# HGRN score products regrouped: the diagonal product ahead of the retention updates, levels 0 to 3 in one run, levels 4 to 6 in another

## The reference, cut to what matters

```python
b = jnp.cumsum(lfc, axis=-2)
diff = b[:, :, :, None, :] - b[:, :, None, :, :]
decay = jnp.exp(jnp.where(causal, diff, -jnp.inf))
scores = jnp.einsum('bhid,bhjd,bhijd->bhij', qc, kc, decay)
```

## Time and profile before

| | |
|---|---|
| median of 3 runs | 1402.32 us (1402.03 to 1403.26) |
| the profiled execution | 1402.38 us |
| its span | 1400.6 us |
| PE busy | 1383.8 us (99%) |
| DVE, ACT, POOL busy | 999.3, 483.7, 368.1 us |
| mean granted TensorE clock | 0.998 |

### The profile page before, as it was taken

The page is one execution under the profiler, slowest core; times in us unless marked ns, Lnnn a source line. Parts: engine busy times, 40 slices in busy tenths (PEclk is TensorE's granted clock), DMA queues, the critical chain, the costliest instruction groups (busy, mean ns, idle before and its releaser), DMA issues.

```text
span 1400.6 us, 24702 instructions
## 1 busy us (share of the span) xinstructions
PE 1383.8 (99%) x10042; PEld 1165.8 (83%) x10042; DVE 999.3 (71%) x1330; ACT 483.7 (35%) x842; POOL 368.1 (26%) x292
## 2 busy tenths in 40 slices
PE   7999999999999999999999999999999999999997
PEld 5788898889888988898889888988898888888886
DVE  5555676667689889988898889877676768532345
ACT  4323243234333333342334333333333344221234
POOL 0000114311532153215321532153206225201220
PEclk9999999999999999999999999999999999999999
DMA  9994442435343535454444454433443357182235
GB/s 387 418 418 161 117 126 69 120 72 139 95 161 108 172 94 178 111 153 119 161 116 140 128 166 114 130 97 106 106 106 86 103 151 278 53 305 93 90 106 210
DMA packets 207735, 212.40 MB, mean 152 GB/s; under 512 B 144256, under 2 KB 156816, under 8 KB 202768
## 3 DMA queue, kind: packets, MB, share of 16 engines
q1 hardware_dynamic: 207600, 210.89, 47.9%
q10 hardware_dynamic: 32, 0.02, 0.0%
HBM read 182.27 MB, written 24.40 MB: 148 GB/s over the span
## 4 chain that ended last, share of the span: by engine, by line
PE 95%; DMA 3%; DVE 1%; SPq 0%; issue 0%; ACT 0%; DVEq 0%; ACTq 0%
PE ps L2122 10%; PE ps L2124 10%; PE ps L2123 10%; PE ps L1957 9%; PE ps L1958 8%; PE ps L1959 8%; PE ps L1933 8%; PE ps L2299 5%; PE ps L2301 5%; PE ps L2300 5%; DMA area<-in_w_mod 2%; PE ps L2139 2%; PE ps L1964 2%; PE ps L1965 2%; PE ps L1966 2%; PE ps L1923 2%
## 5 line engine op out<-in xcount | busy, mean ns | idle before, releaser
L1201 DVE TENSOR_TENSOR w_lo<-area,w_hi 128x1024 fp32r<-128x1024 f32 x143 | 190.3, 1331 | 206.7 <-ACT w_hi L729 206.7
L729 ACT ACTIVATE w_hi<-area 128x1024 fp32r<-128x1024 f32 x143 | 151.5, 1059 | 495.5 <-PE ps L2124 266.1
L2122 PE MATMUL ps<-w_hi,hT_hi 128*128 128x512 f32 x640 | 251.1, 392 | 0.0
L2124 PE MATMUL ps<-w_hi,hT_lo 128*128 128x512 f32 x640 | 249.1, 389 | 0.0
L2123 PE MATMUL ps<-w_lo,hT_hi 128*128 128x512 f32 x640 | 249.0, 389 | 0.0
L1957 PE MATMUL ps<-hT_hi,w_hi 128*128 128x512 f32 x512 | 204.8, 400 | 0.0
L1958 PE MATMUL ps<-hT_lo,w_hi 128*128 128x512 f32 x512 | 199.7, 390 | 0.0
L1959 PE MATMUL ps<-hT_hi,w_lo 128*128 128x512 f32 x512 | 199.6, 390 | 0.0
L2124 PEld LDWEIGHTS ps<-w_hi,hT_lo 128*128 128x128 f32 x640 | 120.1, 188 | 25.2
L2122 PEld LDWEIGHTS ps<-w_hi,hT_hi 128*128 128x128 f32 x640 | 120.2, 188 | 24.3
L2123 PEld LDWEIGHTS ps<-w_lo,hT_hi 128*128 128x128 f32 x640 | 120.2, 188 | 24.1
(11 more groups left out here) (282 smaller groups left out, 2427.7 us busy)
## 6 DMA issues: line engine op xcount, KB each, us to landing
area<-in_w_in SPq DMA_DIRECT2D x144, 512.0 KB, 4.2
area<-in_w_mod SPq DMA_DIRECT2D x26, 1024.0 KB, 12.3
area<-in_w_out SPq DMA_DIRECT2D x38, 512.0 KB, 3.9
gate_raw<-in_w_gate SPq DMA_DIRECT2D x32, 512.0 KB, 4.0
gate_raw<-in_w_mod SPq DMA_DIRECT2D x6, 1024.0 KB, 12.1
o_hi_scratch<-area SPq DMA_DIRECT2D x56, 80.0 KB, 2.4
o_lo_scratch<-area SPq DMA_DIRECT2D x56, 80.0 KB, 2.4
hT_hi<-o_hi_scratch SPq DMA_DIRECT2D x14, 320.0 KB, 7.0
```

The lines of the kernel that those rows point to most:

```text
L729: act.activation(split_weights(h, n)[0], raw[:, n % 3, :], ACT.Copy).then_inc(wt_hi.sem, 1)
L1201: v.tensor_tensor(lo, raw[:, n % 3, :], hi.bitcast(F32), ALU.subtract).then_inc(wt_lo.sem, 1)
L2122: mm(out, hT_hi[:, k, tile_cols(t)], w_hi[:, n % 2, w], start=k == 0, stop=False)
L2124: i = mm(out, hT_lo[:, k, tile_cols(t)], w_hi[:, n % 2, w], start=False, stop=k == KT - 1)
```

## The change

- Product 0 goes behind chunk 0, ahead of the retention updates (`own_scores`), and is placed at DVE's item 0 (`place_own`) instead of item 4. PE waits for that placing ahead of the retention outputs.
- Levels 0 to 3 are one run behind chunk 5 (`early_scores`), levels 4 to 6 one behind chunk 8 (`late_scores`). The gate's four matmuls go ahead of the first run.
- Level 0 uses two matmuls of 64 x 64 a tile in place of four of 32 x 64.
- Levels 2 to 6 and the diagonal are written packed to PSUM (32 columns a tile), and placed by one instruction that repeats them over a tile.
- Each level has a buffer of its own (`decayed`), in areas that belong to retention and key buffers: level 1 in `KL`, 3 in `rqd` and `kts`, 4 and 5 in `ktl`, `rS` and `rope`. So the writers of those wait for the last product (`pe_level`) of the head before, and SP loads the retention states at 14 instead of 6.
- The differences of levels 1 / 2, 3 / 4, 5 / 6 are made at items 3 / 4 / 6 / 7, where they were at items 4 (1, 2), 6 (3, 4) and 8 (5, 6). ACT's exponentials are at 4 (1, 2), 5 (3), 6 (4, 5), 7 (6), the query decays at 4 (1), 5 (2, 3), 7 (4, 5), 8 (6). Placings are at items 6 and 9.
- The last head keeps its single products, with level 0 in the new form.

```diff
+DIFFERENCES = {3: (1,), 4: (2, 3), 6: (4, 5), 7: (6,)}
+OWN_DECAYS = {4: (1,), 5: (2, 3), 7: (4, 5), 8: (6,)}
+DECAYS = {4: (1, 2), 5: (3,), 6: (4, 5), 7: (6,)}
+SCORED, EARLY_PRODUCTS = (5, 8), 5
+PACKED, PACK = 2, TILES * QUAD
...
+        decayed = {0: XE[:, 0], 1: KL, 2: halves(area[:, XE0 - T:XE0 + 5 * T])[:, :, 0:T], 3: halves(area[:, RET1:RET1 + 2 * T]),
+                   4: halves(area[:, KTL0:KTL0 + 2 * T]), 5: halves(area[:, KTL0 + 2 * T:KTL0 + 4 * T]), 6: XE[:, 0]}
...
-                if n == 6 and h is not None:
+                if n == 14 and h is not None:
...
-                    if due(pe_ro, h - 1):
-                        sp.wait_ge(pe_ro.sem, pe_ro.at(h - 1))
+                    if due(pe_level, h - 1):
+                        sp.wait_ge(pe_level.sem, pe_level.at(h - 1))
...
-                        sp.wait_ge(roped.sem, roped.at(h - 1))
+                        sp.wait_ge(pe_level.sem, pe_level.at(h - 1))
...
-                if due(pe_level, h, level):
+                if following is not None and level:
+                    dve.wait_ge(pe_hu.sem, pe_hu.at(h))
+                    if level == LEVELS - 1:
+                        dve.wait_ge(pe_level.sem, pe_level.at(h, EARLY_PRODUCTS))
+                elif due(pe_level, h, level):
...
+            def place_own(h):
+
+                dve.wait_ge(pe_level.sem, pe_level.at(h, 1))
+                scores = ps[:, A, 0:PACK].rearrange("p (t n) -> p t n", n=QUAD).unsqueeze(2).broadcast_to([P, TILES, P // QUAD, QUAD])
+                v.tensor_copy(hsT.rearrange("p (t b n) -> p t b n", t=TILES, n=QUAD), scores).then_inc(h_sT.sem, 1)
...
             def gate_reduced(h):
 
                 b = gate_block(h)
+                pe.wait_ge(h_S.sem, h_S.at(h))
+                pe.wait_ge(h_state.sem, h_state.at(h))
...
-                for c_ in range(4):
-                    if level == 0:
-                        partners = slice(P // 2, P) if c_ < 2 else slice(0, P // 2)
-                    else:
-                        partner = c_ ^ 1 if level == 1 else c_
-                        partners = slice(partner * QUAD, (partner + 1) * QUAD)
-                    rows = slice(c_ * QUAD, (c_ + 1) * QUAD)
+                size = P // 2 if level == 0 else QUAD
+                for c_ in range(P // size):
+                    partner = c_ ^ 1 if level <= 1 else c_
+                    partners = slice(partner * size, (partner + 1) * size)
+                    rows = slice(c_ * size, (c_ + 1) * size)
...
+            def run_scores(h, following, levels):
+
+                for level in levels:
+                    pe.wait_ge(la.sem, la.at(h, level + 2))
+                    pe.wait_ge(lq.sem, lq.at(h, level + 1))
+                    q, keys = level_queries(following, level), level_keys(following, level)
+                    for t in range(TILES):
+                        if level < PACKED:
+                            i = tile_scores(level, ps[:, A, tile_cols(t - 1)] if t else ps[:, DD, 0:P], keys[:, tile_cols(t)], q[:, tile_cols(t)])
+                        else:
+                            i = packed_tile_scores(packed_scores(level)[:, t * QUAD:(t + 1) * QUAD], keys[:, tile_cols(t)], q[:, tile_cols(t)])
+                    i.then_inc(pe_level.sem, 1)
...
                     if n == 0:
+                        own_scores(prev)
                         retention_updates(prev)
                     if n == 1:
+                        pe.wait_ge(h_sT.sem, h_sT.at(prev, 1))
                         retention_outputs(prev, A, BB)
                         chunk_updates(prev)
-                    if n == 3:
-                        level_scores(prev, h, 0)
-                        level_scores(prev, h, 1)
-                    if n in (5, 7, 9):
-                        level_scores(prev, h, n - 3)
-                        if n == 5 and 0 <= gate_block(prev) < GATE_BLOCKS:
+                    if n == SCORED[0]:
+                        if 0 <= gate_block(prev) < GATE_BLOCKS:
                             gate_reduced(prev)
-                        level_scores(prev, h, n - 2)
+                        early_scores(prev, h)
+                    if n == SCORED[1]:
+                        late_scores(prev, h)
```

More of the change, by code:

```diff
@@ L959, in items @@
                     context_columns(h)
-                if prev is not None and n in (4, 6, 8):
-                    decays(prev, n - 3)
-                    decays(prev, n - 2)
+                if prev is not None:
+                    for level in DECAYS.get(n, ()):
+                        decays(prev, h, level)
                 if n == 11:
@@ L1032, in _ @@
             items(CHUNKS - 1, last, None)
-            decays(last, 0)
+            decays(last, None, 0)
             tokens_context(last)
@@ L1475, in chunk_states, with place_packed @@
                     dve.wait_ge(h_S.sem, h_S.at(h, i + 1))
-            def place(h, following, product):
-                scored, placed = pe_level.at(h, (product if following is None else product | 1) + 1), h_sT.at(h, product)
+            def place_packed(h, levels):
+                quads = hsT.rearrange("p (t b n) -> p t b n", t=TILES, n=QUAD)
+                for level in levels:
+                    placed = h_sT.at(h, level)
+                    if not isinstance(h, int):
+                        placed = dve.to_reg(placed)
+                    dve.wait_ge(masks_in.sem, masks_in.at(0))
+                    dve.wait_ge(h_sT.sem, placed)
+                    where = mask(level).rearrange("p (b n) -> p b n", n=QUAD).unsqueeze(1).broadcast_to([P, TILES, P // QUAD, QUAD])
+                    scores = packed_scores(level).rearrange("p (t n) -> p t n", n=QUAD).unsqueeze(2).broadcast_to([P, TILES, P // QUAD, QUAD])
+                    v.copy_predicated(quads, where, scores).then_inc(h_sT.sem, 1)
@@ L1482, in place, with place_late @@
+            def place_late(h):
+                scored = pe_level.at(h)
+                if not isinstance(h, int):
+                    scored = dve.to_reg(scored)
+                dve.wait_ge(masks_in.sem, masks_in.at(0))
+                dve.wait_ge(pe_level.sem, scored)
+                place_packed(h, range(EARLY_PRODUCTS - 1, LEVELS))
+            def place(h, product):
                 if product:
                     dve.wait_ge(masks_in.sem, masks_in.at(0))
-                dve.wait_ge(pe_level.sem, scored)
@@ L1524, in items @@
                         retention_turn(prev)
[L1525 to L1536, removed]
+                    for level in DIFFERENCES.get(n, ()):
+                        differences(prev, h, level)
+                    for level in OWN_DECAYS.get(n, ()):
+                        own_decay(prev, h, level)
+                    if n == 0:
+                        place_own(prev)
+                    if n == SCORED[0] + 1:
+                        place_early(prev)
+                    if n == SCORED[1] + 1:
+                        place_late(prev)
                     if n == 4:
@@ L1673, in _ @@
             hgrn_silu(last, 0)
-            place(last, None, 3)
-            differences(last, 4)
+            place(last, 3)
+            differences(last, None, 4)
             hgrn_silu(last, 1)
@@ L1691, in _ @@
             hgrn_silu(last, 3)
-            place(last, None, 7)
+            place(last, 7)
             hgrn_silu(last, 4)
@@ L1885, in _ @@
             last = HEADS - 1
-            key_decay(last, 0)
+            key_decay(last, None, 0)
             key_factors(last)
             for level in range(1, LEVELS):
-                differences(last, level)
-                key_decay(last, level)
+                differences(last, None, level)
+                key_decay(last, None, level)
             pool.wait_ge(fnw_in.sem, fnw_in.at(0))
```

235 lines of the change are left out of this document (134 added, 101 removed).

## The result

The changed kernel takes 1409.86 us (median of 5 runs, 1409.2 to 1411.51) against 1402.32 before: a ratio of 1.0056, 95% interval 1.0044 to 1.0067. It is slower by 7.5 us, more than twice what can be told from no change, and 3.9 us above the upper end of my range. The profiled execution took 1411.51 us with a span of 1409.7, so its span is 9.1 us longer than before.

What follows compares the result with a forecast made beforehand. PE's own instruction stream was taken as the bound. Its -0.45 us plus 0.4 of stall came to about 0 against the median of 1402.32, so the forecast was 1402.2 us, range 1398.5 to 1406.0.

Steps and rivals of the forecast that it cites:

- the new waits: Whether operands reach PE late at the new places, followed in head 4: 0.4 us of stall in all.
- a key decay: POOL's key decay per level, taken as 2.5 us, so POOL is done at 650.6, 0.9 ahead of level 3.
- the diagonal run: Product 0 on PE ahead of the retention updates, priced at 0.69 us per head with a predecessor.
- The stall: PE waiting for late operands in heads 3 to 6: 0.1 us each, bounds 0 and 2.0 each.
- Rival 3: DVE's query decays of levels 2 and 3 late in heads 3 to 6, 2.0 us each: 1410; chance 0.15.
- PE's price list: PE's score costs: 0.40 us a product, 0.29 a run beside its products, level 0 0.61.
- The early run: Levels 0 to 3 on PE: 2.25 us, seen as about 2.4 from weight matmul to weight matmul.
- the late one: Run of levels 4 to 6 on PE: 1.49 us, seen as 1.6 from weight matmul to weight matmul.
- rivals 1 and 4: Level 0 at 0.31 and inner changes free, 1397.9, chance 0.18; wide strips not overlapping, 1406.6, chance 0.05.
- The inner change of width: Switch between 64-wide and 32-wide strips inside a run on PE: 0.15 us, bounds 0 and 0.29.
- Rival 2: Changes of width drain in full, 0.29 us for each of eleven inner changes: 1403.7; chance 0.12.
- PE's stream: PE's own instruction cost: 0.15 us saved per head, 1.05 in seven, 0.6 back for the gate, -0.45 in all.

Runs made afterwards that it cites:

- x1: Changed kernel with POOL making the key differences of levels 2 and 3 ahead of level 1's key decay: 1401.91 us against 1402.77, ratio 0.9994.
- x3: Changed kernel with DVE's gate step behind item 3 on 8 columns in place of 512, leaving out part of the gate's sum: 1401.48 us, ratio 0.999.
- x9: Changed kernel with DVE's gate step of item 3 ahead of level 1's differences instead of behind them: 1409.86 us, ratio 1.0055.
- x4: Changed kernel with the run of levels 0 to 3 behind chunk 6 in place of chunk 5, its placing one item later: 1408.38 us, ratio 1.004.
- x6: Kernel before the change with only level 0 altered, to two matmuls of 64 stationary columns a tile: 1403.41 us, ratio 1.0007.
- x2: Changed kernel with ACT's exponential of level 2 moved from item 4 to item 5, behind the rounding of chunk 6: 1420.29 us, ratio 1.0124.
- x8: Changed kernel with POOL's differences ahead of its key decay, narrow level 0, and the diagonal product in the early run: 1407.66 us, ratio 1.0039.
- x10: Changed kernel with POOL's differences ahead of its key decay, narrow level 0, and level 3 in the late run: 1404.01 us against 1402.73, ratio 1.0005.

## Why the prediction was wrong

**The step that failed** is in the new waits: "a key decay is 1.20+1.33 = 2.5", with POOL done by 650.6, and from it that ACT's split of chunk 6 waits "to about 645.4, still ahead of DVE". The key decay of level 1 took 5.20 + 0.87 = 6.1 us, as it started beside DVE's unbroken series; ACT's rounding came at 649.9, DVE's split at 650.9, the query decays of levels 2 and 3 from 652.8 to 655.6. In the prediction's own time (1.57 us less) the rounding is at 648.3, 2.9 later than said, and the key decay ends at 645.7 where I had 641.4. Of these 4.3 us, 3.6 are its duration. The other 0.7 is a slip of mine: I took the clocks of head 4 from the before trace and left out the 0.69 of the diagonal run that the change puts ahead of them. The stall I took as 0.1 per gate head, with bounds 0 and 2.0. It measured 1.9, so the upper bound held and the middle did not. I had put a mean duration on an instruction whose neighbour I had just placed beside it: the means of the earlier trace rows come from a schedule in which POOL's key decays met DVE at other moments. x1 takes the wait away by order alone, x3 by taking the gate step away, which moves DVE's series against POOL's start; x9 shows that DVE's end and not POOL's start sets the end, and x4 that ACT's queue carries the loss.

**Rival 3** named the right wait (query decays of levels 2 and 3, heads 3 to 6, 2.0 each, 1410) by the wrong mechanism. It had POOL slow down every DVE step, and I held against it that POOL waits in part of the stretch. DVE was not slowed in the series, where its differences took 0.48; it then stood idle for 5.28 us behind an engine that it had kept out itself. Only from 650.94 on did it run slow beside POOL: 1.90 us for the split in place of 1.22, and 1.44 for each query decay in place of 0.81, 1.9 us in all. That alone makes no wait, as in x1 and x3 the two decays are as slow (2.90 us together) and PE never waits; but with the idle time before it, it adds to how late levels 2 and 3 are. With a chance of 0.15 on the right number, the range should have reached it.

**PE's price list was right.** The diagonal run, said 0.69, is seen in head 2, laid beside the earlier trace rows. From the last query matmul (331.68, the second record of the first line) to the first scan matmul it takes 0.76; less that chunk's step of 0.15, with the 0.07 behind it, that is 0.68:

```profile
331.53 0.46 PE L1996 MATMUL ps<-hT_hi,w_lo 128*128 128x320 f32 x2
331.92 0.56 PE L2267 MATMUL ps<-area 128*32 128x32 f32 x40
332.44 0.91 PE L2213 MATMUL ps<-area 128*128 128x128 f32 x6
333.18 0.39 PE L2214 MATMUL ps<-area 128*128 128x128 f32 x2
```

The six records behind it take 0.74, as in the tail. The early run, said 2.37, took 2.35, the late one, said 1.61, took 1.62; a wide pair of level 0 in the tail comes every 0.058 us, so time goes by the rate of a strip (rivals 1 and 4 fall, the tail's run went from 1.02 to 1.05). The inner change of width, said 0.15, is at most 0.11 (x6). Rival 2, and with it the reading of the Trainium skill's rule on changing the tiling mode (TensorEngine Tiling (Array Packing), Key Properties) that charged a whole 0.29, falls too: an inner change costs under half of that. PE's stream saved 0.24 to 0.28 per plain head where I had 0.15; 0.04 of that is the inner change, the rest, under 0.1, I can't name. In x1, without the waits, it is 0.17 to 0.19, and the gate heads (138.57 to 138.73 us) save nothing, as the sum had it.

**Without the wait the forecast holds.** x1 is the change with POOL's list put in another order: its ratio of 0.9994 makes 1401.5 us of 1402.32, beside my 1402.2, and it is not to be told from the kernel before. The regrouping itself is worth nothing that can be measured; the changed kernel loses some 7 us to one instruction's place in POOL's queue, and in some executions a lowered clock adds to it. None of the versions clearly beats the kernel before.

## What to carry to other kernels

When a change moves an instruction of GpSimd beside a long series of VectorE, take the length of that series as its upper price, not its own mean, and put what other engines wait for ahead of it in the queue. Follow the delay through every in-order queue: here it went from POOL to ACT's exponential, to an unrelated rounding of weights behind it, to DVE and to PE, and mending it anywhere but at its start (x2, x4) only moved it. Joining short runs of very small matmuls saves a fixed 0.2 to 0.3 us a run here, but a run that grows to 160 records or more can pause for longer than that.

## What the runs showed of the hardware

**An instruction of POOL held off.** In heads 3 to 6 of the changed kernel and of every version of it but x3, POOL's first key decay ended 0.73 or 0.74 us after the last instruction of DVE's series, whatever its start: it took 5.11 to 5.21 us (3.56 in x9), with seven (in x9 five) whole DVE instructions passing meanwhile. The Trainium skill (SBUF — State Buffer, SBUF: two separate sides) says that the two engines share a pair of ports under an exclusive lock, which the one that starts first has "for the whole instruction". The traces agree that one engine blocks the other (0.48 against 1.17 us for DVE's difference in x3). By that rule POOL would get in behind the one DVE instruction that was running when it started, and in heads 1, 2 and 7 it did. DVE's timeline in head 2, around the start of POOL's 0.93 us at 362.88:

```profile
362.59 0.48 DVE L1490 TENSOR_TENSOR area<-area 128x320 f32<-128x320 f32 x1
362.99 1.17 DVE L1488 TENSOR_TENSOR area<-area 128x320 f32<-128x320 f32 x1
```

POOL's instruction ended at 363.81, 0.74 us after the first of these two, and the second was held off in turn. In heads 3 to 6 it stayed out for the whole series, against the rule. In x9 it too had started while one of DVE's differences ran (at 642.84, 0.15 before its end). Why it got in behind one instruction in heads 1, 2 and 7 and in x3, and not in the others, stays open.

**The supply of instructions.** Pauses of 1.4 to 2.3 us came only in or right behind runs of at least 160 small records. The Trainium skill (Runtime: NRT & Kernel Launch, Instruction fetch mechanics) has blocks of 16 KiB with 256 instructions, as the count in x8 has, and says that fetching them is mostly hidden; in those runs it looks not to be. PE went on 1.3 to 1.5 us after a block had landed, each time at the same place of a block of 256 records, and only in runs that reach two such places with the fetch begun inside them (x10).

**The clock.** The granted clock fell to 1.2 GHz for 3.4 us at or right behind a pause once in the profile of the changed kernel, three times in that of x2 and once in that of x10, where it cost about 1.6 us (behind a single pause of 2.24 us). It did not fall after the other pauses of the same length: not in x9, which has the changed kernel's, and not after 2.30 us in x8.
